# One transfer for each slot of input weights, the first modulation product moved ahead of the squares, and three parameter blocks transposed among the units

## The reference

```
mod_lat = silu(c) @ w_mod[i] + b_mod[i]          # six rows of 1024: shift, scale, gate, twice
mod_ctx = silu(c_ctx) @ w_mod[i] + b_mod[i]
hc = modulate(rms_norm(x_ctx, g_norm1[i]), csh1, csc1)
h  = modulate(rms_norm(x_lat, g_norm1[i]), sh1, sc1)
u  = h @ w_in       # 1440 columns: 6 query heads, 2 key heads, 2 value heads (64 each),
                    # compressed queries 256, compressed keys/values 128, rope part 32, pool input 256
qg, kg = rms_norm(...), rms_norm(...), then rope on the 256 tokens of x
qm = rms_norm(rms_norm(u_cq, g_cq) @ w_uq);  km, vm from rms_norm(u_ckv, g_ckv) @ w_ukv
mix = concat(attention(qg, kg, vg), attention(qm, km, vm), multiscale_pool(pool_in)) @ w_out
x = x + gt1 * mix;  x = x + gt2 * (relu(modulate(rms_norm(x))  @ w_mlp1) ** 2 @ w_mlp2)
```

## Time and profile before

| | us |
|---|---|
| three runs | 1847.20, 1849.02, 1849.02 (median 1849.02) |
| the profiled execution | 1854.89 |
| its span, first to last instruction | 1853.1 |
| TensorE matmul busy | 1767.0 (95%) |
| VectorE busy | 1107.1 (60%) |
| ScalarE busy | 875.9 (47%) |
| GpSimd busy | 460.0 (25%) |
| mean granted TensorE clock | 0.976 |

### The profile page before, as it was taken

How to read it: one execution, slowest core, us unless ns; L and a number is a source line. 1 busy time by engine, 2 the same in 40 slices (tenths; PEclk the granted TensorE clock), 3 DMA queues, 4 the chain that set the end, 5 groups by cost and what they waited for, 6 DMA issues and landing times.

```text
span 1853.1 us, 28648 instructions
## 1 busy us (share of the span) xinstructions
PE 1767.0 (95%) x10804; PEld 1440.7 (78%) x10804; DVE 1107.1 (60%) x1971; ACT 875.9 (47%) x1741; POOL 460.0 (25%) x864
## 2 busy tenths in 40 slices
PE   5898999899999998989899989999999899999998
PEld 3352454588888886736899989899899898898998
DVE  4218841687777633285555568577555585785555
ACT  2326631332323243274455556566554475674542
POOL 1015101000000002150000016128772152187730
PEclk9899999899999999999999999999999999999999
DMA  8510631255554441210445543543335344432351
GB/s 283 182 64 28 227 138 46 91 182 182 182 176 174 174 100 38 97 40 1 161 179 180 178 164 107 186 150 120 137 137 182 137 149 170 149 138 101 129 195 55
DMA packets 140020, 255.27 MB, mean 138 GB/s; under 512 B 14942, under 2 KB 21740, under 8 KB 139884
## 3 DMA queue, kind: packets, MB, share of 16 engines
q1 hardware_dynamic: 138886, 251.16, 38.6%
q0 software_dynamic: 704, 2.10, 0.3%
q10 hardware_dynamic: 294, 0.18, 0.0%
HBM read 252.38 MB, written 1.05 MB: 137 GB/s over the span
## 4 chain that ended last, share of the span: by engine, by line
PE 91%; DVE 4%; ACT 2%; issue 1%; DMA 1%; SPq 1%; POOL 0%; DVEq 0%; ACTq 0%; POOLq 0%
PE ps L1163 18%; PE ps L1165 18%; PE ps L1164 18%; PE ps L1188 10%; PE ps L1042 2%; PE ps L1304 2%; PE ps L1403 2%; PE ps L1405 2%; PE ps L1404 2%; PE ps L1330 2%; PE ps L1316 1%; PE ps L1069 1%; PE ps L1137 1%; PE ps L1113 1%; PE ps L1483 1%
## 5 line engine op out<-in xcount | busy, mean ns | idle before, releaser
L1592 ACT ACTIVATE big_r<-ring 128x1024 fp32r<-128x1024 f32 x198 | 209.0, 1058 | 391.0 <-PE ps L1165 377.0
L2014 DVE TENSOR_TENSOR big_r<-ring,big_r 128x1024 fp32r<-128x1024 f32 x198 | 245.2, 1240 | 229.8 <-ACT big_r L1592 229.5
L1164 PE MATMUL ps<-big_r 128*128 128x256 f32 (+1 forms) x1088 | 360.5, 331 | 0.0
L1163 PE MATMUL ps<-hT_r,big_r 128*128 128x256 f32 (+1 forms) x848 | 270.0, 318 | 0.0
L1165 PE MATMUL ps<-hT_r,big_r 128*128 128x256 f32 (+1 forms) x848 | 265.4, 313 | 0.0
L909 POOL TENSOR_TENSOR sq<-sq 128x256 f32<-128x256 f32 (+1 forms) x30 | 36.6, 1220 | 777.6 <-ACT sq L1552 777.6
L1164 PEld LDWEIGHTS ps<-big_r 128*128 128x128 f32 x1088 | 206.8, 190 | 19.1
L1188 PE MATMUL ps<-hT,ring 128*128 128x512 f32 (+1 forms) x544 | 191.7, 512 | 18.0 <-DMA ring<-in_w_in 10.7
L1163 PE MATMUL ps<-big_r 128*128 128x256 f32 (+1 forms) x592 | 195.8, 331 | 1.4 <-DVE big_r L2174 1.4
L1165 PE MATMUL ps<-big_r 128*128 128x256 f32 (+1 forms) x592 | 194.7, 329 | 0.0
L1188 PEld LDWEIGHTS ps<-hT,ring 128*128 128x128 f32 x544 | 105.3, 195 | 101.4 <-issue 82.0
(11 more groups left out here) (312 smaller groups left out, 4184.9 us busy)
## 6 DMA issues: line engine op xcount, KB each, us to landing
ring<-in_w_in SPq DMA_DIRECT2D x42, 2048.0 KB, 7.8
ring<-in_w_mlp SPq DMA_DIRECT2D x32, 2048.0 KB, 7.7
ring<-in_w_mod SPq DMA_DIRECT2D x24, 2048.0 KB, 7.9
ring<-in_w_out SPq DMA_DIRECT2D x4, 2048.0 KB, 8.3
ring<-in_w_out_a SPq DMA_DIRECT2D x4, 2048.0 KB, 8.6
ring<-in_w_out_b SPq DMA_DIRECT2D x4, 2048.0 KB, 7.7
ring<-in_w_o SPq DMA_DIRECT2D x4, 2048.0 KB, 8.1
ring<-in_w_in SPq DMA_DIRECT2D x12, 256.0 KB, 4.7
```

What stands on the lines that cost most here:

```text
L1163: mm(b[:, 0:T], w_hi[:, k, :], hi(k), start=(k == 0), stop=False)
L1164: mm(b[:, 0:T], w_hi[:, k, :], lo(k), start=False, stop=False)
L1592: act_fn(hi, raw, ACT.Copy).then_inc(hi_ready, 1)
L2014: V.tensor_tensor(lo, raw, hi.bitcast(F32), ALU.subtract).then_inc(lo_ready, 1)
```

## The change

It does four things. The host permutes the query columns of `w_in` before the launch, so that `win` 0 is one ordinary transfer like the others. TensorE does modulation product 0 before the squares and products 1 to 3 behind them. The parameter blocks 1, 2 and 3 are transposed inside the units kr, p0 and p1, into bank 2, right behind the unit's product, and copied and scaled by VectorE at the same units. The first transposition of the modulation row still comes after product 1.

```diff
+PARAMS_AT = {"kr": 1, "p0": 2, "p1": 3}
...
             for n, b in enumerate(banks):
                 take((tag, name, n), b)
+            if tag == ("a", 0) and name in PARAMS_AT:
+                take(("prm", PARAMS_AT[name]), 2)
...
-            for s in range(1, 2 * DEPTH):
-                take(("prm", s), s)
...
-    transfers = [7 if k[0] == "win" and k[2] == 0 else 1 for k in slots]
...
+    landed_at = [16 * (n // RING + 1) for n in range(len(slots))]
...
-                if key[0] == "win" and key[2] == 0:
-
-                    for h in range(GQ):
-                        pos = 2 * (h % 3) + h // 3
-                        sp.dma_start(ring[:, r, :, pos * HD:(pos + 1) * HD], src[:, :, h * HD:(h + 1) * HD])\
-                          .then_inc(slot_landed[r], 16)
-                    sp.dma_start(ring[:, r, :, GQ * HD:SLOT], src[:, :, GQ * HD:SLOT]).then_inc(slot_landed[r], 16)
-                else:
-                    sp.dma_start(ring[:, r, :, 0:src.shape[2]], src).then_inc(slot_landed[r], 16)
+                sp.dma_start(ring[:, r, :, 0:src.shape[2]], src).then_inc(slot_landed[r], 16)
...
                     pe.wait_ge(const_landed, 32)
+                    pe.wait_ge(silu_made, 1)
+                    mod_products(0, range(KC))
                     squares((tag, "n1"), cc("ones"), P, TOK, KC)
...
-                    pe.wait_ge(silu_made, 1)
-                    for n in range(MOD_FIRST):
+                    for n in range(1, MOD_FIRST):
                         mod_products(n, range(KC))
-                        if n:
-                            mod_transposed(n - 1, n, "modA", 0, MOD_FIRST)
+                        mod_transposed(n - 1, n, "modA", 0, MOD_FIRST)
...
+                    if i == 0 and name in PARAMS_AT:
+                        params_transposed(PARAMS_AT[name])
-                    elif name[:2] == "qm":
+                    if name[:2] == "qm":
...
-                if i == 0:
-                    for s in range(1, 2 * DEPTH):
-                        params_transposed(s)
...
                     if kind == "norm":
                         apply_norm(tag, name)
+                    if tag == ("a", 0) and name in PARAMS_AT:
+                        params_copied(PARAMS_AT[name])
+                        params_scaled(PARAMS_AT[name])
...
-                if i == 0:
-                    for s in range(1, 2 * DEPTH):
-                        params_copied(s)
-                        params_scaled(s)
...
+    w_in = arrays["in_w_in"]
+    q = w_in[:, :, 0:GQ * HD].reshape(DEPTH, D, 2, GQ // 2, HD).transpose(0, 1, 3, 2, 4).reshape(DEPTH, D, GQ * HD)
+    arrays["in_w_in"] = np.ascontiguousarray(np.concatenate([q, w_in[:, :, GQ * HD:]], axis=2))
```

## The result

The kernel after takes **1842.91 us** (median of 20 runs, 1837.72 to 1849.05), the kernel before in the same comparison 1849.02 (20 runs, 1844.7 to 1856.6). The ratio is 0.9966 with an interval of 0.9954 to 0.9978: faster by 6.3 us, between 4.1 and 8.5. Forecast was 14.1. The direction was right; less than half of the size came.

What follows compares the result with a forecast made beforehand. TensorE was taken as the bound except while awaiting the first input weights and during VectorE's norms and parameter blocks before the attention. −10.0 − 6.35 − 1.5 + 3.8 = −14.1 us gave 1834.9 us, range 1831.0 to 1840.0.

Steps and rivals of the forecast that it cites:

- the start of q0: First input product on TensorE: single weight transfer and early product 0 together start it at 44.15, not 54.17, 10.0 us gained.
- Part 1: Opening: first input weights in one transfer, so q0 waits only for hT's first chunk at 47.2; worth 7.0 us.
- Part 2: Opening: modulation product 0 ahead of the squares frees the fourth modulation slot sooner; product 3 starts 3.05 us earlier.
- The waits at kr: TensorE waits for bank 2 at the moved parameter transposes, and later at qm0; cost 3.8 us, between 1.0 and 6.0.
- Rival 1: The clock falls at the kr pause; price 2.2 us, saving 11.9, time 1837.1; chance 0.15.
- Part 3: Ahead of the attention: moving parameter blocks among the units removes their VectorE stretch before the first row maximum; worth 6.35 us.
- Part 4: Attention's opening: without the pause TensorE's clock stays full; worth 1.5 us, between 0 and 2.3.
- Rival 3: The attention's opening gives nothing; saving 12.6 us, time 1836.4; chance 0.06.
- Carried to the end undiminished: After the attention TensorE is the chain almost to the end, without transfers on it, so the front's whole gain is kept.
- Rivals 2, 5 and 6: 2: modulation unmoved, saving 11.1, 0.10; 5: one transfer no earlier, saving 4.1, 0.03; 6: clock stays half after kr, 1863, 0.02.

Runs made afterwards that it cites:

- seven transfers: The kernel after with the first input weights again fetched in seven transfers, the other changes kept: 1847.21 us, 3.1 us faster than before.
- free banks: The kernel after with the three parameter blocks transposed into banks 1, 2 and 3 instead of bank 2 each time: 1837.63 us, 12.6 us faster than before.
- rows spread: free banks with seven of the eight later modulation rows transposed between the attention's value products instead of behind it: 1830.87 us, 18.5 us faster than before.
- before filled: The kernel before with filler matmuls of constants, results overwritten, where TensorE pauses: 1851.89 us, 0.2 us faster than before.
- after filled: The kernel after with filler matmuls of constants, results overwritten, where TensorE pauses: 1838.48 us, 15.0 us faster than before.
- the last kernel: rows spread with filler matmuls ahead of product 0 (three), q0 (four) and vm1 to vm3 (one each): 1827.19 us, 21.8 us faster than before.

## Why the prediction was wrong, step by step

**The step that failed** is the start of q0, 54.17 to 44.15, "10.0 us", together with the sentence that the median is 5.9 below the profiled execution "for reasons outside this stage". The end point was, if anything, too late (43.38 in after, 42.1 on average in six kernels). The starting point was one execution: four executions of before have q0 at 54.2, 50.8, 46.1 and 51.5, 50.65 on average, so the gain by profiles is 8.6. These four took 1851.2 on average, 2.2 above the median of 1849.02 and 1.0 above the medians of before in their own comparisons; as q0's start makes most of the spread among them, between 6 and 8 is left for the median run. That last step is an estimate. The parameters-only kernel, which has the opening of before, bears it out: q0 at 54.6 in an execution of 1854.74, 7.9 above its median. The prediction counted the late weights twice: once as a gain and once, at 5.9, as time that the median does not have.

**Part 1**, "7.0": 2.4 alone. The mechanism stood (one issue of 0.37, no DMA wait ahead of q0). From the mean start of 50.65 the 47.2 worked out would have been 3.5; in the one profile of this kernel the clock fall at product 3 cost 3.3 us. Such a fall costs nothing where the weights are late, and comes into the open when they are early.

**Part 2**, "3.05": right in its instants within 1 us, and 3.0 by medians. By profiles it was worth 8.5 beside the transfer alone, since it also removes the pause behind which product 3 was slow in that one. The squares ended 0.9 earlier than worked out, as the clock was back when they began, at 22.0, and not at 24.2.

**The waits at kr**, "3.8": 5.6 (21.7 for 16.1). The pause was 2.58 where 2.7 was said, and the sum of waits right to 0.1 with the clock held (3.9). **Rival 1**, to which 0.15 was given, was true in all three profiles that have the stall (after, parameters only, seven transfers: 21.7, 21.4, 21.6), and its price, 2.2, was about right (1.8). Its argument, "a pause of 2.76 us left it at 1.00, one of 3.46 cost it", took one execution for a rule: in the fast execution of before (46.15), 2.79 lost it ahead of the same instruction, and 3.63 ahead of the squares left it at 1.00.

**Part 3**, "6.35": 4.9 in after (41.7 for 46.6, with the clock at 0.55 from 168 on) and in the two other kernels with the stall and no fillers, 6.3 with free banks, 5.1 with the rows spread, 6.1 filled (against before filled). The mechanism is right. What it missed is that the four vm units have VectorE's norms as their bound, with pauses of 0.3, 1.2 and 1.2 on TensorE, behind which the clock fell in after. In the profile of before, with the same pauses, it did not; there a fall would have been beside the parameters' scaling.

**Part 4**, "1.5": 0.6 from the row maximum to the modulation transposes (82.6 for 83.2), 0.4 with free banks. Rival 3, nothing at all, is nearer than the forecast. The port rule of the Trainium skill ("SBUF — State Buffer", section "Who interferes with whom") would have VectorE's scalings longer beside GpSimd. No run here tests it: the four first scalings took 3.25 us in before, 2.82 in after and 3.98 with free banks, and GpSimd was busy for 94 or 95% of that stretch in all three. The prediction's premise that its sums "now lie wholly beside the attention's opening" does not set after apart: in before GpSimd was busy there too, 7.53 of the 8 us from 182 on.

**Carried to the end undiminished**: no. The stretch behind the attention moves by 3 us from one execution to the next with the clock. In the profile of after it took 2 more than the mean of the four of before, and in that of the transfer with product 0 as much; whether it does so on average is not shown by so few profiles.

The attention was to begin at 169; it began at 172.2. The terms as measured, 6 to 8 for q0, 4.9, 0.6, less 5.6, make 6 to 8, beside the 6.3 [4.1, 8.5] of the runs. Rivals 2, 5 and 6 were not seen: the modulation moved, the transfer was earlier, and the clock came back within p0.

**What stays open**: why the same 512 KB land in 5.9 us in one execution and 11.8 in another; why the same pause lowers the clock in one execution and not in another; and how much of q0's lead the first two parts keep. The ratio gives them 4.4 [2.0, 6.8], where q0 in the profiles is 9.4 earlier (50.65 to 41.3). In the profile of that kernel, near its median at 1844.03, the lead over the mean of the four of before is 8.7 at the row maximum and 6.4 at the output products; less the 1.0 to 2.2 by which those four lie above the median, 4 to 5.5 is left, inside the interval.

## What to carry to other kernels

Price a stall by several profiled executions, and find the stage that a slow profiled run owes its difference from the median to before that difference is subtracted. Where a wait is removed, look for what could lie hidden beside it: here a fall of the clock. Where fillers are to hold the clock, read the mean clock of all runs and not of the profiled one alone. Where a transpose or any small step is moved among the products of a TensorE-bound stretch, give it a bank that is free at that time: a pause of 2.6 us cost 4.8.

## What was not expected of the hardware

- The same pause does not always have the same effect, and a longer one can leave the clock where a shorter one lowers it. Ahead of product 3, pauses of 2.76, 2.96 and 2.92 us left the products at 1.92, and behind 2.79 and 2.72 they took 3.21 and 3.64. Ahead of product 0 in the kernels with it first, 2.90 and 2.98 (after, seven transfers) were followed by 3.35 and 3.64, and 3.14 and 3.19 (free banks; transfer and product 0) by 1.92 and 1.93. At kr 2.58 lost the clock in each of three kernels.
- During the 64 matmuls of 128x2 behind the attention, which follow each other without a pause, the granted clock fell to 0.50, sooner in one execution than in another: they took 9.3 us in before and 11.9 in after (5.75 + 3.55, 8.32 + 3.55).
- The spread of a kernel's runs differs with the program: 11 to 12 us over 20 runs of before and of after, 4.7 over six of free banks, 2.0 over six of after filled, 2.6 over six of the last kernel (a few runs show less of a spread than 20 do). Fillers alone did not bring it: before filled still spread over 9.5 in 12.
